# Order of the moving columns in the score and value stages, and two tiles at other SBUF places

## The reference

```python
def chunk(args):                      # hc: 128 tokens of the normalised input
    hc, ec, gc = args                 # ec, gc: 128 chosen experts of a token, and their gates
    u = peer_u[ec]
    a = jax.nn.gelu(jnp.einsum("ckd,cd->ck", u, hc).astype(jnp.float32)) * gc
    vv = peer_v[ec]
    return jnp.einsum("ck,ckd->cd", a.astype(vv.dtype), vv)
```

## Time and profile before

| | us |
|---|---|
| two runs | 1581.11 and 1935.71 |
| their median | 1758.41 |
| the profiled execution | 1579.2 |
| its span, first to last instruction | 1577.1 |
| PE busy in the span | 1563.8 (99%) |
| PE weight loads busy | 1472.5 (93%) |
| DVE, ACT, POOL busy | 1069.8, 881.2, 883.7 |

### The profile page before, as it was taken

How to read it: one execution, slowest core, us unless ns; L and a number is a source line. 1 busy time by engine, 2 the same in 40 slices (tenths; PEclk the granted TensorE clock), 3 DMA queues, 4 the chain that set the end, 5 groups by cost and what they waited for, 6 DMA issues and landing times.

```text
span 1577.1 us, 33476 instructions
## 1 busy us (share of the span) xinstructions
PE 1563.8 (99%) x12568; PEld 1472.5 (93%) x12568; DVE 1069.8 (68%) x1867; ACT 881.2 (56%) x1251; POOL 883.7 (56%) x413
## 2 busy tenths in 40 slices
PE   9999999999999999999999999999999999999998
PEld 8999899999999999998888888889999999999998
DVE  7998743879933777778888666676937484455522
ACT  6567766454454444444444445557677654676653
POOL 8786468978886000000000244458875689888886
PEclk9999999999999999999999999999999999999999
DMA  6564335555555555555555655566543356665563
GB/s 222 173 197 154 107 122 192 194 178 195 188 187 189 171 177 171 178 166 175 179 178 163 219 190 190 195 195 188 178 140 111 118 165 190 195 197 190 188 196 124
DMA packets 86217, 277.03 MB, mean 176 GB/s; under 512 B 11232, under 2 KB 18160, under 8 KB 86128
## 3 DMA queue, kind: packets, MB, share of 16 engines
q1 hardware_dynamic: 85712, 274.76, 54.0%
q0 software_dynamic: 272, 1.05, 0.2%
q10 hardware_dynamic: 144, 0.00, 0.0%
HBM read 274.73 MB, written 1.05 MB: 175 GB/s over the span
## 4 chain that ended last, share of the span: by engine, by line
PE 92%; issue 2%; DVE 2%; POOL 2%; ACT 2%; DMA 0%; SPq 0%; DVEq 0%; ACTq 0%; POOLq 0%
PE gemm L683 35%; PE gemm L986 22%; PE gemm L688 18%; PE aux L1272 4%; PE gemm L817 3%; PE aux L966 2%; POOL w_lo L466 1%; PE gemm L704 1%; PE gemm L729 1%; ACT w_hi L1368 1%; PE gemm L1272 1%; PE aux L936 0%; PE gemm L803 0%; PE gemm L710 0%; PE gemm L746 0%
## 5 line engine op out<-in xcount | busy, mean ns | idle before, releaser
L466 POOL TENSOR_TENSOR w_lo<-raw,w_hi 128x1024 fp32r<-128x1024 f32 (+1 forms) x330 | 789.4, 2401 | 282.9 <-ACT w_hi L1368 279.1
L1368 ACT ACTIVATE w_hi<-raw 128x1024 fp32r<-128x1024 f32 (+1 forms) x492 | 514.9, 1048 | 560.5 <-PE gemm L683 310.2
L683 PE MATMUL gemm<-h_hi,w_hi 128*128 128x256 f32 x2096 | 289.2, 280 | 1.1 <-ACT w_hi L1368 1.0
L683 PE MATMUL gemm<-h_lo,w_hi 128*128 128x256 f32 x2144 | 289.9, 277 | 0.0
L688 PE MATMUL gemm<-h_hi,w_lo 128*128 128x256 f32 x2096 | 284.6, 278 | 2.4 <-POOL w_lo L466 1.5
L683 PEld LDWEIGHTS gemm<-h_lo,w_hi 128*128 128x128 f32 x2144 | 266.0, 188 | 0.3 <-issue 0.2
L683 PEld LDWEIGHTS gemm<-h_hi,w_hi 128*128 128x128 f32 x2096 | 261.3, 188 | 4.2 <-issue 1.6
L466 DVE TENSOR_TENSOR w_lo<-raw,w_hi 128x1024 fp32r<-128x1024 f32 x162 | 195.7, 1223 | 102.0 <-ACT w_hi L1368 101.7
L688 PEld LDWEIGHTS gemm<-h_hi,w_lo 128*128 128x128 f32 x2096 | 259.8, 188 | 4.8 <-POOL w_lo L466 3.4
L986 PE MATMUL gemm<-w_hi,act_parts 128*128 128x512 f32 x1008 | 251.0, 391 | 0.4 <-ACT act_parts L1569 0.4
L986 PEld LDWEIGHTS gemm<-w_hi,act_parts 128*128 128x128 f32 x1008 | 188.2, 188 | 38.8 <-issue 0.5
(11 more groups left out here) (436 smaller groups left out, 2044.4 us busy)
## 6 DMA issues: line engine op xcount, KB each, us to landing
raw<-in_w_u SPq DMA_DIRECT2D x128, 512.0 KB, 3.5
raw<-in_w_ev SPq DMA_DIRECT2D x128, 512.0 KB, 3.6
raw<-in_w_up SPq DMA_DIRECT2D x48, 512.0 KB, 3.6
raw<-in_w_gate SPq DMA_DIRECT2D x24, 512.0 KB, 3.7
raw<-in_w_down SPq DMA_DIRECT2D x24, 512.0 KB, 3.5
raw<-in_w_conv_in SPq DMA_DIRECT2D x16, 512.0 KB, 4.4
raw<-in_w_peer_q SPq DMA_DIRECT2D x16, 512.0 KB, 4.0
raw<-in_w_branch SPq DMA_DIRECT2D x24, 288.0 KB, 2.8
```

The lines of the kernel that those rows point to most:

```text
L466: eng.tensor_tensor(w_lo[v][:, 0:n], raw[c.raw][v][:, 0:n], w_hi[v][:, 0:n], ALU.subtract).then_inc(lo_ready[v], 1)
L683: mm = pe.matmul(spread(out), w[:, k, :], spread(act_part[:, k, :]), start=(n == k == 0), stop=False)
L1368: act.activation(w_hi[v][:, 0:n], raw[c.raw][v][:, 0:n], ACT.Copy).then_inc(hi_ready[v], 1)
```

## The change

Three things:

1. In `product_tile` the 256-column order is no longer always `spread`. `column_order` looks up the chunk: in the score stage each of the eight pairs of slot and tile v gets an order of its own; all other stages keep `spread`.
2. In `expert_values` each pair of slot and tile gets an order too, where there was none. `last_values` keeps the plain one.
3. The 32 unused bytes ahead of `h_hi` are gone, so it begins at 57472, a multiple of 128. `h_lo` begins at 65680, 16 bytes past one. All tiles behind them stay where they were.

```diff
-        sb("ahead_of_h", [P, 8])
         h_hi = sb("h_hi", [P, KD, T], F32R)
         with nc.sbuf_tensor("mem_sq", [P, KD, T], F32) as mem_sq:
             pass
-        h_lo = sb("h_lo", [P, KD, T], F32R)
-        sb("behind_h", [P, 8])
+        h_low_room = sb("h_low_room", [P, KD * T + 16], F32R)
+        h_lo = h_low_room[:, 4:4 + KD * T].rearrange("p (k t) -> p k t", t=T)
...
+        def rounds(columns_falling=False, rounds_falling=False):
+
+            def turn(tile):
+                v = tile.rearrange("p (j g c) -> p g j c", g=4, c=4)
+                v = v[:, ::-1] if rounds_falling else v
+                return v[:, :, ::-1, :] if columns_falling else v
+            return turn
+
+        def together(parts, falling=True):
+
+            def turn(tile):
+                v = tile.rearrange("p (g j c) -> p j g c", g=parts, c=4)
+                return v[:, ::-1] if falling else v
+            return turn
+
+        def pairs(tile):
+
+            return tile.rearrange("p (j g c) -> p g j c", g=2, c=8)
+
+        def plain(tile):
+
+            return tile
+
+        SCORE_ORDER = ((rounds(), together(2)), (together(4), rounds(False, True)),
+                       (rounds(True, True), plain), (pairs, together(2, False)))
+        VALUE_ORDER = ((rounds(), rounds(False, True)), (rounds(True), rounds(True, True)),
+                       (together(2), together(4)), (plain, rounds()))
+
+        def column_order(c, v):
+
+            for name, orders in (("u", SCORE_ORDER), ("ev", VALUE_ORDER)):
+                first = plan[name][0].index
+                if first <= c.index < first + len(plan[name]):
+                    return orders[(c.index - first) % BANKS][v]
+            return spread
...
-                        mm = pe.matmul(spread(out), w[:, k, :], spread(act_part[:, k, :]), start=(n == k == 0), stop=False)
+                        mm = pe.matmul(turn(out), w[:, k, :], turn(act_part[:, k, :]), start=(n == k == 0), stop=False)
...
-                                mm = pe.matmul(gemm[2 * half + tt][:, :], a[:, c.raw, v, tt * P:(tt + 1) * P],
-                                               w[v][:, half * (D // 2):(half + 1) * (D // 2)],
+                                mm = pe.matmul(turn(gemm[2 * half + tt][:, :]), a[:, c.raw, v, tt * P:(tt + 1) * P],
+                                               turn(w[v][:, half * (D // 2):(half + 1) * (D // 2)]),
```

More of the change, by code:

```diff
@@ L676, in product_tile @@
                 w = by_k(w_hi[v], m, n=steps)
+                turn = column_order(c, v)
                 for n, act_part in enumerate(x):
@@ L687, in product_tile @@
                 for k in range(steps):
-                    mm = pe.matmul(spread(out), w[:, k, :], spread(x[0][:, k, :]), start=False, stop=(k == steps - 1))
+                    mm = pe.matmul(turn(out), w[:, k, :], turn(x[0][:, k, :]), start=False, stop=(k == steps - 1))
                 mm.then_inc(tile_done[v], 1)
```

## The result

The change takes 1613.46 us (two runs, 1612.74 and 1614.18). Against the lower run of before the ratio is 1.0207, with a 95% interval of 1.019 to 1.0225: it is slower, and whether by more than 2% isn't settled, since the interval holds 2%. The second run of before, 1935.71 us, was a disturbed one; 54 later runs of the same kernel lie between 1579.6 and 1583.7 us. The forecast was 1575.1 us, the range 1564 to 1590. It was wrong, in sign as well.

A forecast was written before the change was run, and what follows sets the result against it. TensorE's matmul pace was taken to bound the kernel. Value stage -7.1, plain +2.0, pairs +1.0, other score orders and places 0 made -4.1 us on 1579.2: 1575.1 us, range 1564 to 1590.

The forecast's parts named there:

- What bounds the kernel: Whole kernel: TensorE busy 99%, waiting only 0.6 us over both changed stages, so only the pace of matmuls can move.
- Score stage, five other orders: Score stage, 1920 matmuls in other stepped orders: 0, from -9.6 us (excess gone) to +10.2 us (as bad as plain).
- Value stage, -5.3 ns on 1332 matmuls: Value stage, stepped instead of plain order: excess per matmul falls from 10.3 to 5.0 ns, -7.1 us in all.
- 10.3 ns of excess: Value stage: time per 512-column matmul beyond its columns and a fixed 3.1 ns, the most another order could win.
- Plain and pairs with 256 columns: Score stage, 384 matmuls each: plain costs +5.3 ns a matmul, +2.0 us; pairs stands between, +1.0 us.
- The places, 0: All 6336 matmuls reading h_hi and h_lo as moving operand: new places change nothing, bounds -3.2 and +20 us.
- Rival 4: Score and value stages: far jumps of `together` halve the stream, +195 us, about 1770 us; chance 0.04.
- The rule on PSUM: Value stage: non-contiguous PSUM access slows matmuls; stepping would gain nothing and cost up to 10.0 ns each, +13.3 us.
- Rival 1: Both stages: order does nothing, excess goes by the column; 1579.2 us, with the places 1576 to 1582; chance 0.31.

## Why the prediction was wrong, point by point

**What bounds the kernel** was right: PE 99% busy before and after, its waits in the two stages 0.6 us before and 0.4 after, and the whole change acted through the pace of two stages.

**Score stage, five other orders, "0, with ends of -9.6 and +10.2 us".** This is the step that failed. The ends came from the only excess the trace had, and I reckoned an order could at worst be as bad as plain. Three of these five were `together`, and cost 13.2, 22.2 and 14.1 ns a matmul, two and a half to four times the end of 5.3. Instead of 0 the five were worth about +20 us.

**Value stage, -5.3 ns on 1332 matmuls.** The same mistake for 384 of them: +24.8 and +43.2 ns. For true rounds the sign was right and the size too large: in the change they gave from -3.6 ns to +0.1 (both turns), by themselves about -1.6 with plain rounds and -3.4 with the best turned ones over the whole stage. Of the 10.3 ns of excess a third is the most that an order won there. That the excess belongs to the load of the next tile no run shows; no experiment touched the load.

**Plain and pairs with 256 columns, +5.3 and +2.6 ns.** Measured +4.4 and +3.5. Right within a nanosecond, with some luck in it: it was reckoned from the load, which nothing bears out, and by the same reckoning rounds should have won 5.3 ns in the value stage too. What the runs show is that columns in a row are slower to read than 64-byte steps, at both lengths (119.3 against 115.3 ns, 228.9 against 225.3).

**The places, 0.** Right: +0.05%, within the interval. The bounds of -3.2 and +20 us were too wide; the upper one took L817's slow pace for h as the moving operand, where in L817 the weights move and h is the stationary tile. `up` was to be at 114.8 ns and was at 114.2, which the other profiles show to be one of two paces.

**Rival 4, far jumps are slow, 0.04.** This is what happened, though not for its reason: the price goes by multiples of 256 bytes and not by the distance, and only on the side of SBUF. Its chance was far too low. I had written that 64 bytes already leave a new line each time, and held that against it; but 256-column matmuls with steps of 64 and of 256 bytes both do, and have 115.0 and 134.9 ns. The trace of before has no row for an order like `together`. A walk of which the diff shows steps of 256, 512 and 1024 bytes, with no row for any, should have had a chance of its own and a price from 0 up, not the price of halving the stream, which gave an absurd 1770 us and so looked easy to dismiss. Its sign, a single pair of slot and tile with a pace far from its neighbours, is what the profile after shows. The point from which it decides was well put: 16 ns per 256 columns; measured were 16.5 on the mean in the score stage and 17.0 per 256 columns in the value stage, and the ratio is 1.0207.

**The rule on PSUM.** The Trainium skill, "SBUF — State Buffer", section "Door 1", has non-contiguous PSUM accesses slow matmuls significantly. With 16-byte pieces no run shows that: written with steps of 256 or 512 bytes, PSUM left the pace at 115.3 to 115.6 ns, where rounds have 115.3. The measurement decides. The wish in the same section of the Trainium skill for at least two hits in each 16-byte line is kept by all these orders, which read four columns of 4 bytes in a row, and doesn't set them apart.

**Rival 1's ground.** From two independent reads, of the weights and of the moving columns, the prediction went on to say that no order of the columns would matter. That doesn't follow, and it isn't so: with PSUM written in rounds throughout, the reading alone takes the pace from 115.3 to 135.0 ns. Whether the load of the weights has a part in it isn't shown either way.

## What to carry to other kernels

When float32r columns are read out of order, look at the distance between one 16-byte piece and the next: steps that are multiples of 256 bytes cost about 0.4 to 0.5 ns each, 64 bytes cost nothing and are even better than no step. Only the side that reads SBUF matters, so with 16-byte pieces the pattern of the PSUM output can follow the layout (steps of 64, 256 and 512 bytes were tried). And where a diff brings a pattern that no row of the trace has, leave room in the range for it instead of bounding it by the nearest pattern. A gain of 1 or 2 ns in the pace of one stage wants more than one profile and a look at both halves of the stage.

## What the runs showed of the hardware

- A piece of 16 bytes read right after one at a multiple of 256 bytes costs some 0.39 to 0.49 ns: 13.2 / 32 = 0.41, 22.2 / 48 = 0.46, 24.8 / 64 = 0.39, 43.2 / 96 = 0.45, and (278.9 - 223.6) / 112 = 0.49. At the granted clock of 1.00, its level of 2.4 GHz, a cycle is 0.42 ns, so it looks like one lost cycle; that reading is my own estimate. Pieces of 32 and 64 bytes with far steps cost 5.9 to 8.4 ns for 256 columns with no such neighbours, so there is a second part that this rule doesn't have.
- 16 bytes less in the step take most of it away (256 to 240: 134.7 to 117.2 ns).
- With each piece read twice in a row, so that half as many pieces are read, 256 columns take 111.6 ns, 3.2 less than rounds (114.8): part of the excess over the columns' own 106.7 ns goes with how many different pieces are read.
- The pace of equal matmuls with equal tiles at equal places differs by 1 to 3 ns with 256 columns between stretches and runs (`up` at the new places: 113.8 to 114.2 in three profiles, 115.3 to 115.4 in four; score stage in rounds at the new places: 113.8 to 116.8), and in one run by up to 5 ns with 512 columns from loop to loop (plain rounds: 222.7 to 227.8). Some orders don't have it: in the second half of the value stage columns in a row stay at 226.6 to 226.8 ns (one loop 227.5), rounds walked from their end at 223.0 to 223.8.
